# One more ordering of a two-way recurrence interleaved with attention: decay sums, products, scores and calls change places

## The reference, cut to what matters

```python
def wkv7_scan(r, w, k, v, a, b, reverse):
    def step(state, inp):
        r_t, w_t, k_t, v_t, a_t, b_t = inp
        sa = jnp.einsum('bhvk,bhk->bhv', state, a_t)
        state = (state * w_t[:, :, None, :] + sa[..., None] * b_t[:, :, None, :]
                 + v_t[..., None] * k_t[:, :, None, :])
        return state, jnp.einsum('bhvk,bhk->bhv', state, r_t)
    ...
# attention, per block of 128 queries
s = (jnp.einsum('bqhd,bkhd->bhqk', qn_b, k_nope)
     + jnp.einsum('bqhd,bkd->bhqk', qr_b, k_rope))
p = jax.nn.softmax(s.astype(jnp.float32) * scale, axis=-1)
return jnp.einsum('bhqk,bkhd->bqhd', p.astype(v.dtype), v)
# in rwkv7_branch
fwd = direction(dlo_f, glo_f, w0[0], w2[0], g2[0], False)
bwd = direction(dlo_b, glo_b, w0[1], w2[1], g2[1], True)
return fwd + bwd
```

## Time and profile before

| | us |
|---|---|
| median of 3 runs | 3447.28 |
| lowest, highest | 3444.87, 3449.14 |
| the profiled execution's own time | 3440.47 |
| its span in the profile | 3438.7 |
| PE busy | 3199.9 (93%) |
| DVE busy | 2036.8 (59%) |
| ACT busy | 1073.5 (31%) |
| mean granted TensorE clock | 0.963 of full |

### The profile page before, as it was taken

One profiled execution on the slowest core, in us unless ns is written; L12 is line 12 of the kernel. 1 busy time (PEld: TensorE's weight loads), 2 busy tenths in 40 slices (PEclk: granted clock), 3 DMA queues, 4 the chain that ended last, 5 costly groups with the idle time before them and its releaser, 6 DMA issues.

```text
span 3438.7 us, 52047 instructions
## 1 busy us (share of the span) xinstructions
PE 3199.9 (93%) x22004; PEld 2553.4 (74%) x22004; DVE 2036.8 (59%) x3230; ACT 1073.5 (31%) x1526; POOL 315.1 (9%) x306
## 2 busy tenths in 40 slices
PE   7898999688888887999999999999998999999999
PEld 6686787566666666877888888877755888778887
DVE  3655454367677667534454454447979887645445
ACT  3222334344444443213111111122234333423332
POOL 0123342000000001310000000000000000000000
PEclk9999999799899988999999999999999999999999
DMA  3242665334333333430111111111101223223222
GB/s 140 76 142 79 204 222 195 64 78 103 84 98 80 82 79 121 145 126 28 60 49 49 49 49 48 43 45 37 37 25 49 81 93 109 74 74 123 98 98 74
DMA packets 93527, 301.86 MB, mean 88 GB/s; under 512 B 10352, under 2 KB 38640, under 8 KB 70768
## 3 DMA queue, kind: packets, MB, share of 16 engines
q1 hardware_dynamic: 79104, 246.63, 23.0%
q0 software_dynamic: 14192, 51.91, 4.4%
HBM read 241.35 MB, written 57.15 MB: 87 GB/s over the span
## 4 chain that ended last, share of the span: by engine, by line
PE 75%; DVE 11%; issue 4%; ACT 4%; DMA 3%; POOL 2%; SPq 1%; DVEq 0%; ACTq 0%; POOLq 0%
PE ps L2370 24%; PE ps L308 20%; PE ps L466 6%; PE ps L1724 3%; PE ps L2195 2%; PE ps L2512 2%; DMA Dn<-nbs 2%; PE ps L1713 2%; PE ps L1316 2%; PE ps L2030 1%; PE ps L437 1%; DVE Yh L2539 1%; PE ps L974 1%; PE ps L2390 1%; SPq L1667 1%
## 5 line engine op out<-in xcount | busy, mean ns | idle before, releaser
L2370 PE MATMUL ps<-Hh,whi 128*128 128x512 f32 x1600 | 498.1, 392 | 0.0
L284 ACT ACTIVATE whi<-raw 128x2048 fp32r<-128x2048 f32 x139 | 265.6, 1911 | 626.5 <-PE ps L308 310.5
L288 DVE TENSOR_TENSOR wlo<-raw,whi 128x2048 fp32r<-128x2048 f32 x139 | 318.8, 2294 | 172.5 <-ACT whi L284 171.9
L2370 PEld LDWEIGHTS ps<-Hh,whi 128*128 128x128 f32 x1600 | 300.3, 188 | 68.0 <-issue 6.2
L2370 PE MATMUL ps<-Hh,wlo 128*128 128x512 f32 x800 | 311.3, 389 | 0.0
L2370 PE MATMUL ps<-aHh,whi 128*128 128x512 f32 x512 | 199.8, 390 | 3.6 <-DVE xT L2716 2.5
L308 PE MATMUL ps<-Hlo,whi 128*128 128x512 f32 x656 | 202.0, 389 | 0.0
L308 PE MATMUL ps<-Hhi,wlo 128*128 128x512 f32 x656 | 201.9, 389 | 0.0
L308 PE MATMUL ps<-Hhi,whi 128*128 128x512 f32 x656 | 201.9, 389 | 0.0
L2370 PE MATMUL ps<-aLh,whi 128*128 128x512 f32 x512 | 199.2, 389 | 0.0
L2370 PE MATMUL ps<-aHh,wlo 128*128 128x512 f32 x512 | 199.2, 389 | 0.0
(11 more groups left out here) (378 smaller groups left out, 6244.4 us busy)
## 6 DMA issues: line engine op xcount, KB each, us to landing
raw<-in_panels SPq DMA_DIRECT2D x139, 1024.0 KB, 4.8
rwf<-F POOLq DMA_DIRECT2D x16, 1280.0 KB, 6.5
L<-rwf SPq DMA_DIRECT2D x16, 1024.0 KB, 5.0
L<-rwf SPq DMA_DIRECT2D x64, 256.0 KB, 4.2
Dn<-nbs SPq DMA_DIRECT2D x128, 128.0 KB, 5.0
gts<-so POOLq DMA_DIRECT2D x16, 512.0 KB, 3.2
gl<-gts SPq DMA_DIRECT2D x32, 256.0 KB, 3.3
rwt<-so POOLq DMA_DIRECT2D x15, 512.0 KB, 3.0
```

The source lines that it names most:

```text
L284: e.activation(whi[i % 2][:, :], raw_of(i)[:, :], AF.Copy).then_inc(*a_hi.up(i))
L288: e.tensor_tensor(wlo[i % 2][:, :], raw_of(i)[:, :], whi[i % 2][:, :].bitcast(F32), OP.subtract).then_inc(*v_lo.up(i))
L2370: m = e.matmul(ap, W[wi][:, kc, n0:n0 + 128], mov[mi][:, kc, :], start=x == 0 and q == 0, stop=x == len(kcs) - 1 and q == 2)
```

## The change

Five edits.

1. In cum, PE does sum 1 ahead of sum 0 and signals each by itself; ACT does E3 as soon as sum 1 is there, then E1 and E2.
2. In mul, DVE makes the products in the order At, Rt, Bt, Kt, and Rt and Bt wait for E1 and E2 by themselves. PE's turns and ACT's copies take the same order.
3. In attention's half 0, S(u) comes ahead of O on PE.
4. In a slot, direction 1's call comes ahead of direction 0's; row1 comes ahead of post2, and row2 ahead of post3; the attention halves are dealt out by other tables FRONT and EACH (the same 17 and 16 in number).
5. In the tail, panel WO is loaded two slots earlier, and split one slot earlier on ACT and on DVE.

```diff
--- before.py
+++ after.py
@@ -1299,15 +1299,14 @@
             b0 = wtake(e, d, s, "cum0", (a, s, "E2"))
             b1 = wtake(e, d, s, "cum1", (a, s, "E3"))
             b2 = wtake(e, d, s, "D", (a, s, "eD"))
-            for n, ap in enumerate((b0, b1)):
+            for n, ap in ((1, b1), (0, b0)):
                 e.matmul(ap, trir[:, 2 * d + n, :], x.sghi[:, :], start=True, stop=False)
-                m = e.matmul(ap, trir[:, 2 * d + n, :], x.sglo[:, :], start=False, stop=True)
-            m.then_inc(*t.up(s, "cum"))
+                e.matmul(ap, trir[:, 2 * d + n, :], x.sglo[:, :], start=False, stop=True).then_inc(*t.up(s, "cum", n))
             for p in range(4):
                 m = e.matmul(b2[:, 2 * p:2 * p + 2], sg[:, 128 * p:128 * (p + 1)], K("ones2", 2), start=True, stop=True)
             m.then_inc(*t.up(s, "D"))
         if c == "turn":
-            for name, sig, empty in (("At", v, a), ("Bt", v, a), ("Rt", v, a), ("Kt", v, a)):
+            for name, sig, empty in (("At", v, a), ("Rt", v, a), ("Bt", v, a), ("Kt", v, a)):
                 ap = wtake(e, d, s, name, (empty, s, name + "T"))
                 e.wait_ge(*sig.by(s, name))
                 for p in range(4):
@@ -1448,19 +1447,20 @@
                 e.wait_ge(*t.by(s - 1, "Y", 5))
             e.activation(x.sghi[:, :], sg, AF.Copy).then_inc(*a.up(s, "sghi"))
         if c == "cum":
-            e.wait_ge(*t.by(s, "cum"))
+            e.wait_ge(*t.by(s, "cum", 1))
+            e.activation(x.E3[:, :], wring.bank(d, s, "cum1"), AF.Exp, scale=-KAPPA).then_inc(*a.up(s, "E3"))
+            e.wait_ge(*t.by(s, "cum", 0))
             if s:
                 e.wait_ge(*t.by(s - 1, "H"))
             e.activation(x.E1[:, :], wring.bank(d, s, "cum0"), AF.Exp, scale=-KAPPA).then_inc(*a.up(s, "E1"))
             e.activation(x.E2[:, :], wring.bank(d, s, "cum0"), AF.Exp, scale=KAPPA).then_inc(*a.up(s, "E2"))
-            e.activation(x.E3[:, :], wring.bank(d, s, "cum1"), AF.Exp, scale=-KAPPA).then_inc(*a.up(s, "E3"))
             e.wait_ge(*t.by(s, "D"))
             if s >= 2:
                 e.wait_ge(*v_w[d].by(s - 2, "S", 1))
             e.activation(x.sc[:, 8 * (s % 2):8 * (s % 2) + 8], wring.bank(d, s, "D")[:, 0:8], AF.Exp,
                          scale=-KAPPA).then_inc(*a.up(s, "eD"))
         if c == "turn":
-            for name in ("At", "Bt", "Rt", "Kt"):
+            for name in ("At", "Rt", "Bt", "Kt"):
                 e.wait_ge(*t.by(s, name))
                 if s and name == "Rt":
                     e.wait_ge(*v_w[d].by(s - 1, "RG", 1))
@@ -1519,8 +1519,10 @@
                                    op1=OP.mult).then_inc(*v.up(s, "At"))
             if s:
                 e.wait_ge(*t.by(s - 1, "H"))
+            e.wait_ge(*a.by(s, "E1"))
+            e.tensor_tensor(x.Rt[:, :], r_, x.E1[:, :], OP.mult).then_inc(*v.up(s, "Rt"))
+            e.wait_ge(*a.by(s, "E2"))
             e.tensor_tensor(x.Bt, pairs(b_), pairs(x.E2[:, :]), OP.mult).then_inc(*v.up(s, "Bt"))
-            e.tensor_tensor(x.Rt[:, :], r_, x.E1[:, :], OP.mult).then_inc(*v.up(s, "Rt"))
             e.tensor_tensor(x.Kt[:, :], k_, x.E2[:, :], OP.mult).then_inc(*v.up(s, "Kt"))
         if c == "scores":
             for half in range(2):
@@ -1701,6 +1703,16 @@
 
     def att_pe(e, u, c):
         g, k, j, h = u // 2, u // 16, (u // 2) % 8, u % 2
+        if c == 0 and u < 64:
+            if u % 16 == 0:
+                e.wait_ge(*d_kp.by(k))
+            if h == 0:
+                e.wait_ge(*d_qb.by(g))
+            if u:
+                e.wait_ge(*a_at.by("E", u - 1))
+            for half in range(2):
+                m = e.matmul(bank[4 + half], Qb[g % 3][:, h, :], Kp[k % 2][:, h, hs(half)], start=True, stop=True)
+            m.then_inc(*t_at.up("S", u))
         if c == 0 and h and g >= 1:
             w = g - 1
             e.wait_ge(*a_at.by("PT", 2 * w + 1))
@@ -1713,16 +1725,6 @@
                     m = e.matmul(bank[7][64 * n:64 * n + 64, 128 * (w % 4):128 * (w % 4) + 128],
                                  Vp[(w // 8) % 2][:, i, 64 * n:64 * n + 64], PT[:, i, n, :], start=i == 0, stop=i == 7)
             m.then_inc(*t_at.up("O", w))
-        if c == 0 and u < 64:
-            if u % 16 == 0:
-                e.wait_ge(*d_kp.by(k))
-            if h == 0:
-                e.wait_ge(*d_qb.by(g))
-            if u:
-                e.wait_ge(*a_at.by("E", u - 1))
-            for half in range(2):
-                m = e.matmul(bank[4 + half], Qb[g % 3][:, h, :], Kp[k % 2][:, h, hs(half)], start=True, stop=True)
-            m.then_inc(*t_at.up("S", u))
         if 1 <= u <= 64:
             w = u - 1
             e.wait_ge(*a_at.by("P", w))
@@ -1788,10 +1790,10 @@
                 kv_sp(e, u // 16 + 1)
 
     BEFORE = ("cum", "mul", "turn", "scores", "PV", "Nc")
-    BETWEEN = ('S0', 'S1', 'post1', 'row0', 'post2', 'row1', 'post3', 'row2', 'row3', 'row4', 'row5')
+    BETWEEN = ("S0", "S1", "post1", "row0", "row1", "post2", "row2", "post3", "row3", "row4", "row5")
     AFTER = ("spread", "X", "Y4", "X4", "Y5", "X5", "WU", "RG", "OH")
     LATER, AHEAD, BACK, UNITS = 13, 24, 3, 132
-    FRONT, EACH = (1, 2, 2, 1, 1, 2, 2, 1, 2, 1, 1, 1, 0), (1, 0, 1, 1, 1, 1, 0, 0, 1, 1, 0, 1, 1, 0, 0, 0, 1, 0, 1, 1, 0, 0, 1, 1, 1, 0, 1)
+    FRONT, EACH = (1, 2, 2, 1, 1, 2, 2, 1, 2, 0, 1, 1, 1), (0, 0, 1, 1, 1, 1, 0, 0, 1, 1, 0, 0, 1, 1, 0, 1, 1, 0, 1, 0, 0, 1, 1, 1, 1, 0, 1)
 
     def way_calls():
         made = [(0, "split")]
@@ -1813,7 +1815,7 @@
         calls = way_calls()
         n, made, at = len(calls) + LATER, [], 0
         for k in range(n):
-            for d in range(2):
+            for d in (1, 0):
                 i = k - LATER * d
                 if d == 0 and i >= len(calls) - 3:
                     i = max(i - BACK, len(calls) - 4)
@@ -1823,7 +1825,7 @@
             for _ in range(min(more, UNITS - at)):
                 made.append((2, at // 2, at % 2))
                 at += 1
-            if k >= n - 18:
+            if k >= n - 20:
                 made.append((3, k - n + 18, 0))
         return made
 
@@ -1941,9 +1943,10 @@
         e.wait_ge(*v_w[0].by(7, "S", 1))
 
     def tail_sp(e, i):
-        if i == 0:
+        if i == -2:
             att_over(e)
             panel_sp(e, WO)
+        if i == 0:
             for d in range(2):
                 e.wait_ge(*v_w[d].by(7, "Bt"))
                 e.wait_ge(*v_w[d].by(7, "Kt"))
@@ -1968,7 +1971,7 @@
             e.activation(mix[n][:, hs(h)], aring.bank("ya", n, h), AF.Copy).then_inc(*a_mx.up("ya", n, h))
 
     def tail_act(e, i):
-        if i == 1:
+        if i == 0:
             att_over(e)
             panel_act(e, WO)
         if i == 2:
@@ -1987,7 +1990,7 @@
             panel_act(e, WO + 2)
 
     def tail_dve(e, i):
-        if i == 2:
+        if i == 1:
             att_over(e)
             panel_dve(e, WO)
         if i == 4:
@@ -2008,7 +2011,7 @@
             e.wait_ge(*t_at.all())
             e.wait_ge(*v_at.all())
             e.wait_ge(*a_at.all())
-        for y in range(PIECES[i - 1] if i else 0, PIECES[i]):
+        for y in range(PIECES[i - 1] if i > 0 else 0, PIECES[i] if i > 0 else 0):
             piece_pe(e, y // 4, y % 4)
 
     FIRST = [[(0, 0), (0, 2), (1, 0)], [(1, 2), (2, 0), (2, 2)], [(3, 0), (3, 2), (0, 1)], [(1, 1), (2, 1), (3, 1)]]
```

## The result

| | before | after |
|---|---|---|
| median (runs) | 3446.07 (4) | 3403.55 (4) |
| lowest, highest | 3441.97, 3449.14 | 3401.31, 3405.46 |
| span of the profiled execution | 3438.7 | 3399.5 |

The ratio is 0.9877 (95% interval 0.986 to 0.9894): 42.5 us faster. The forecast was 3390, 57 faster, with a range of 3350 to 3428.

What follows compares the result with a forecast made beforehand. The prediction took one chain, handed between three engines in list order, to bound the kernel. Halves -61, clock +12, first slots -4, tail -1.7 made -55 from 3447.3: 3392, said as 3390, range 3350 to 3428.

Steps and rivals of the forecast that it cites:

- Half B: Each of six halves B: 36.2 us of PE work, 7.0 idle and 2.0 for low clock, 45.2 in sum.
- half A (38 to 42): Sign for half A, turn to turn; the sum was 36.5 us of work plus 3.0 idle, 39.5 at full clock.
- the stretch of 14: Sign: the stage cut at the starts of the 14 turns after the first, near 590 us, 652.97 before.
- the new wait at WU: In half B, WU waits for X5's add, which stands behind row0 on DVE: 1 to 2 us.
- the 12 us: Half A's turn and first S at half clock after PE's wait, in half of the cases: 7 x 3.5 x 0.5.
- (a): Half A: Nc goes ahead of the maximum and Y4 follows X, so both chains start 5 us or more earlier.
- (b): Half A: the S ahead of WU moves behind it and covers the copies that RG waited 1.37 us for.
- The rival of full clock throughout: Short waits cost no clock in the new order: 3368, or 3350 with half B at 42; chance 0.20.
- the 2.0 of half B: 2.0 us added to each half B for low clock after PE waits of 2.3 to 2.7.
- a bound of 61: Attention's maximum on DVE starts 1.9 us sooner for each odd u: at most 32 x 1.9 = 61 of 99.0 us.
- 4 us in the ramp: The first slots, with one direction alone, gain about 4 us from attention's scores going ahead of its values.
- The slower rival: Row0's data comes late and holds both halves: slower from about 5 us late, some 3470 at 7; chance 0.09.

Runs made afterwards that it cites:

- e5: The changed kernel with the 8 reads of Dn cut from 128 KB to 8 KB each (output wrong, for time alone): ratio 0.9752 to the kernel before.
- e4: The changed kernel with panel WO loaded and split where it was before the change: ratio 0.9863 to the kernel before.

## Why the prediction was right, and where a term was off

**The sign and the mechanism.** The loop did hang on the order in which three engines hand work to each other. The forecast waits came and went where they were put: At, scores, X, OH and row0. Half B was forecast at 45.2 and measured 44.9. Of the signs named ahead, half A (38 to 42) and the stretch of 14 (near 590, measured 615.6) were missed, and the new wait at WU was 1.0 at most and not 1 to 2. (The 590 leaves out the 12 us that the prediction's own sum took back for the clock.)

**Half A, the term that was missing.** Forecast 39.5 (plus 0.35 in the later steps) at full clock, measured 43.3. The walk through the list was right: (a) Nc starts 12.5 us after the turn, (b) the idle ahead of RG, read as a wait for the copies of WU that an S would cover, is gone in all seven, and the idle before OH is 0.8 for the forecast 0.9. What the sum put at nothing, without a reason, is PE waiting for its own instructions: 1.2 to 2.9 us in each half A, 13.0 in the seven, and behind six of these stops a stretch at half clock (at 1064.10 it makes WU and S longer by 1.7 and 0.9 us). With small reads (e5) half A is 39.6. The kernel before had none of these stops in its halves A, so no row could warn of them; they came with the new order.

**The sum of the thirteen halves.** Forecast were 61 less 12 for the clock, 49; measured are 40.5. The seven halves A are 27 us over their 39.5. Some 10 of it is the half clock after the turn, for which 12 were set aside, and the other 17 had no term. Half B and the later steps, 6.6 lower than forecast, make up for a part. So the total, 42.5 us in place of 57, came as near as it did partly because terms that were a little too high stood against one that was missing.

**The clock after direction 0's turn.** Taken in half of the cases, with 12 us in sum. In the 4 us from each of these seven turns the granted clock was 0.57 to 0.68 in six, and 1.0 in one, behind idle times of 1.45 to 1.76; in the seven turns of direction 1, with 0 to 0.81 idle ahead, it was 1.0 each time. Over 5 us the six have 0.66 to 0.68, so each lost 1.6 to 1.7 us, 10 in all: the 12 was nearly right in sum by two errors, too few cases and too high a price. The rival of full clock throughout is out. Its lower figure, 3350, also counted the 2.0 of half B twice: half B at 42 is 1.2 under 43.2, and six times that below 3368 is 3361.

**Who earns it.** The prediction gave edit 3 no term of its own beyond a bound of 61 and its 4 us in the ramp, and put the rest under edit 4. Alone, edit 3 gives 22 us and edit 4 nothing; in the new order edit 3 is worth 38. The walk through the list had all five edits in it, so its waits came out and its shares did not. Edits 1 and 2, put at 7, measured 18 alone and 11 in the whole.

**Ramp and tail.** 4 us were forecast for the first slots; 9.1 came in the ramp, and 3.8 and 2.8 were lost at its two ends, which leaves 2.5. PE's wait for the panel fell from 8.40 to 4.95, not to 6 to 7:

```profile
1306.44 1.19 PE L2033 MATMUL ps<-oahi,whi 128*128 128x512 f32 x2 [4.95 <-DVE wlo L288]
```

In e4, without edit 5, it is 6.3, so only 1.4 of the fall is the edit's, and in the time it is worth nothing that can be measured.

**The slower rival.** Row0's data did not come late: 14.5 us in 6 waits, 8.2 of it in the first step, against 19.3 in 8. It would have had to be 5 us in each half.

## What to carry to other kernels

Idle time whose releaser is "issue" is not one thing, and each case needs a look. Here it was first a wait for the later of two copies, which showed in the end of that copy 0.07 us ahead of the waiter in every period, and which the order could cover; then it was PE waiting for its own instructions, which showed in a fixed count of instructions between the stops, and which no wait on the page foretold. A new order moves both. Parts of a reordering should be priced one at a time as well as together: a list walked with all edits in it gives the waits, but here the order was worth nothing without the swap of two calls that looked like a detail. When two chains share a slot, ask for each slot whose result is wanted first: one order for all of them cost 20 us that three turned slots gave back.

## What the runs showed of the hardware

- With 8 reads of 128 KB under way (q1 at 98.4% of the 16 engines) PE stood still for 1.2 to 2.9 us inside a run of matmuls that waited for nothing; with reads of 8 KB these stops of half A went (e5).
- All 102 such stops of over 0.35 us in the stage, in the fourteen traces, stand ahead of PE's instruction 256 n + 193, and each ends 1.3 to 2.0 us after a 16 KB packet of the instruction queue q8 landed. The packet ahead of the stop at 1061.31 took 1.73 us among Dn's reads, the next one 0.88.
- The granted clock fell in nearly each case behind a short stop: 1.45 to 1.76 us idle before a turn gave 0.57 to 0.68 over the next 4 us in six of seven, and in the seven turns with 0.81 and less it was 1.0. That these stops are the cause is not shown, as no run changed them alone. The Trainium skill (TensorE: Matmul & The Clock Gate, Part 1) warns of long idle gaps and also tells of a kernel in which short ones, coming often, made the clock swing; the trace fits the second, with gaps of a microsecond and a half.
